# Who makes the sums of the down weights: GpSimd takes the four sums of each quarter, VectorE three low parts of each pass

## The reference

```
h = x + 0.5 * swiglu(rmsnorm(x), w_gate, w_up, w_down)          # first feed-forward stage
p = rmsnorm(h) @ w_in ; state-space group and short convolution  # mixer
h = h + concat(s_out, c_out) @ w_out
h = h + 0.5 * swiglu(rmsnorm(h), w_gate2, w_up2, w_down2)        # second feed-forward stage
y = rmsnorm(h)
swiglu(x, wg, wu, wd) = (silu(x @ wg) * (x @ wu)) @ wd           # inner width 2816
```

## Time and profile before

| | us |
|---|---|
| median of 3 runs | 1780.46 (1779.91 to 1780.72) |
| the profiled execution | 1779.56 |
| its span, first to last instruction | 1777.7 |
| TensorE busy | 1761.6 (99%), 11953 matmuls |
| VectorE busy | 1316.3 (74%), 2429 instructions |
| ScalarE busy | 652.3 (37%), 1281 instructions |
| GpSimd busy | 644.3 (36%), 669 instructions |
| granted clock of TensorE, mean | 0.998 |

### The profile page before, as it was taken

One profiled execution on the slowest core, in us unless ns is written; L12 is line 12 of the kernel. 1 busy time (PEld: TensorE's weight loads), 2 busy tenths in 40 slices (PEclk: granted clock), 3 DMA queues, 4 the chain that ended last, 5 costly groups with the idle time before them and its releaser, 6 DMA issues.

```text
span 1777.7 us, 31737 instructions
## 1 busy us (share of the span) xinstructions
PE 1761.6 (99%) x11953; PEld 1749.4 (98%) x11953; DVE 1316.3 (74%) x2429; ACT 652.3 (37%) x1281; POOL 644.3 (36%) x669
## 2 busy tenths in 40 slices
PE   8999999999999999999999999999999999999998
PEld 7999999999999999999999999999999999999998
DVE  7658878777877876823775769977887797788766
ACT  7411333333333333533112545333333333333324
POOL 2688232332333232203995221223233332323321
PEclk9999999999999999999999999999999999999999
DMA  6132111111111111355113501111111112111112
GB/s 174 36 131 84 54 54 48 55 48 57 46 54 54 48 54 43 143 128 128 48 42 110 174 14 54 47 56 48 54 48 54 54 43 60 48 54 48 54 49 96
DMA packets 162647, 119.75 MB, mean 67 GB/s; under 512 B 10258, under 2 KB 156242, under 8 KB 161988
## 3 DMA queue, kind: packets, MB, share of 16 engines
q1 hardware_dynamic: 157012, 110.10, 20.9%
q0 software_dynamic: 864, 5.28, 0.9%
q10 hardware_dynamic: 4624, 2.36, 0.6%
HBM read 102.01 MB, written 15.72 MB: 66 GB/s over the span
## 4 chain that ended last, share of the span: by engine, by line
PE 96%; DVE 2%; ACT 1%; issue 0%; DVEq 0%; POOL 0%; POOLq 0%
PE bank_pair L1128 26%; PE bank_pair L1130 25%; PE bank_pair L1129 25%; PE bank_down L1128 6%; PE bank_down L1130 6%; PE bank_down L1129 6%; DVE HT L2298 1%; DVE XL L2321 1%; PE bank_pair L1542 0%; PE bank_pair L1515 0%; PE bank_pair L1638 0%; PE bank_pair L1534 0%; PE bank_pair L1236 0%; PE bank_down L1278 0%; DVE S L2315 0%
## 5 line engine op out<-in xcount | busy, mean ns | idle before, releaser
L1128 PE MATMUL bank_pair<-XHM,U_hi 128*128 128x344 f32 x720 | 230.5, 320 | 0.2 <-DVE XLM L2343 0.2
L1129 PE MATMUL bank_pair<-XLM,U_hi 128*128 128x344 f32 x720 | 229.7, 319 | 0.0
L1130 PE MATMUL bank_pair<-XHM,U_lo 128*128 128x344 f32 x720 | 229.7, 319 | 0.0
L2549 DVE SCALAR_TENSOR_TENSOR HT<-bank_pair,HT 128x344 f32<-128x344 f32 x378 | 186.2, 508 | 51.0 <-PE bank_pair L1130 50.8
L3206 POOL TENSOR_TENSOR U_lo<-AST,U_hi 128x512 fp32r<-128x512 f32 x74 | 106.0, 1435 | 266.1 <-ACT U_hi L1702 266.1
L1128 PE MATMUL bank_pair<-XH,U_hi 128*128 128x344 f32 x608 | 194.1, 319 | 0.0
L1130 PE MATMUL bank_pair<-XH,U_lo 128*128 128x344 f32 x608 | 194.1, 319 | 0.0
L1129 PE MATMUL bank_pair<-XL,U_hi 128*128 128x344 f32 x608 | 194.0, 319 | 0.0
L1128 PE MATMUL bank_pair<-XH,WH 128*128 128x344 f32 x576 | 186.7, 324 | 5.0 <-DVE XL L2321 4.9
L1130 PE MATMUL bank_pair<-XH,WL 128*128 128x344 f32 x576 | 184.2, 320 | 0.0
L1129 PE MATMUL bank_pair<-XL,WH 128*128 128x344 f32 x576 | 184.2, 320 | 0.0
(11 more groups left out here) (398 smaller groups left out, 4922.7 us busy)
## 6 DMA issues: line engine op xcount, KB each, us to landing
DQ_raw<-in_ffn_w_down SPq DMA_DIRECT2D x52, 256.0 KB, 2.7
U_raw<-in_ffn_w_gate SPq DMA_DIRECT2D x40, 256.0 KB, 3.0
AST<-in_ffn_w_gate SPq DMA_DIRECT2D x40, 256.0 KB, 2.9
U_raw<-in_ffn_w_up SPq DMA_DIRECT2D x40, 256.0 KB, 3.3
AST<-in_ffn_w_up SPq DMA_DIRECT2D x40, 256.0 KB, 2.9
RAW<-in_w_in SPq DMA_DIRECT2D x16, 512.0 KB, 4.0
DQR<-in_ffn_w_down SPq DMA_DIRECT2D x25, 256.0 KB, 2.6
X<-in_x_prompt SPq DMA_DIRECT2D x8, 512.0 KB, 8.6
```

What stands on the lines that cost most here:

```text
L1128: pe.matmul(out, wh, xh, start=first, stop=False, skip_group_check=onto)
L1129: pe.matmul(out, wh, xl, start=False, stop=False, skip_group_check=onto)
L1130: return pe.matmul(out, wl, xh, start=False, stop=last, skip_group_check=onto)
L2549: dve.scalar_tensor_tensor(ht, STEP_BANKS[STEP_BANK[n]][:, 0:TW], 0.5, ht, ALU.mult, ALU.add).then_inc(pair_free, 1)
```

## The change

`mix_quarter` moves from VectorE's list to GpSimd's, with the same waits and semaphores. In return the low parts of A21, A22 and S4 move from GpSimd's list to VectorE's, in each of the 36 passes. In VectorE's even pass they stand at chunks 12 (A22) and 21 (S4), and at chunk 40 for the A21 of the coming odd pass; in its odd pass A22 stands behind `h_lo2(p, 0)` in M1, S4 behind the first product sum in M2, and the A21 of the coming even pass in M3. In GpSimd's list of the odd pass two quarters stand ahead of S1, one ahead of S4 and one behind it.

```diff
--- before.py
+++ after.py
@@ -2514,19 +2514,6 @@
                 hi, lo, raw = quarter(n)
                 dve.tensor_tensor(lo[:, :], raw[:, :], f(hi[:, :]), ALU.subtract).then_inc(dq_ready, 1)
 
-            def mix_quarter(n):
-                dve.wait_ge(dq_in[QUARTERS[n]], quarter_loads(n))
-                if n >= 2:
-                    dve.wait_ge(pair_full, sums_end(n - 2))
-                w = quarter(n)[2][:, :].rearrange("p (k m n) -> p k m n", k=2, m=2)
-                s, done = SR[n % 2], 4 * mixed_quarters(n)
-                dve.tensor_tensor(s[:, S1 - S1, :], w[:, 0, 1], w[:, 1, 1], ALU.add).then_inc(dq_mixed, 1)
-                dve.tensor_tensor(s[:, S3 - S1, :], w[:, 0, 0], w[:, 0, 1], ALU.subtract).then_inc(dq_mixed, 1)
-                dve.wait_ge(dq_mixed, done + 1)
-                dve.tensor_tensor(s[:, S2 - S1, :], s[:, S1 - S1, :], w[:, 0, 0], ALU.subtract).then_inc(dq_mixed, 1)
-                dve.wait_ge(dq_mixed, done + 3)
-                dve.tensor_tensor(s[:, S4 - S1, :], w[:, 1, 0], s[:, S2 - S1, :], ALU.subtract).then_inc(dq_mixed, 1)
-
             def sums_lo(n):
                 dve.wait_ge(ds_hi, mixed_quarters(n) + 1)
                 dve.tensor_tensor(SL[n % 2][:, :, :], SR[n % 2][:, :, :], f(SH[n % 2][:, :, :]), ALU.subtract
@@ -2644,32 +2631,34 @@
                                 quarter_lows(4 * p - 3)
                             if chunk == 11:
                                 unit_lo(t, S2)
+                            if chunk == 8 and t == FIRST[e] + 2:
+                                unit_lo(t, A21)
+                            if chunk == 12:
+                                unit_lo(t, A22)
                             if chunk == 13:
                                 unit_lo(t, S1)
-                            if chunk == 14:
-                                mix_quarter(4 * p - 2)
                             if chunk == 16:
                                 c11(t)
                             if chunk == 18:
                                 quarter_lows(4 * p - 2)
                             if chunk == 20:
                                 unit_lo(t, S3)
-                            if chunk == 23:
-                                mix_quarter(4 * p - 1)
+                            if chunk == 21:
+                                unit_lo(t, S4)
                             if chunk == 26:
                                 quarter_lows(4 * p - 1)
                             if chunk == 29:
                                 c22(t)
                             if chunk == 33:
                                 unit_lo(t + 1, A11)
-                            if chunk == 32 and p not in LAST_PAIR:
-                                mix_quarter(4 * p)
                             if chunk == 35:
                                 unit_lo(t + 1, S1)
                             if chunk == 37:
                                 c12(t)
                             if chunk == 39:
                                 unit_lo(t + 1, A12)
+                            if chunk == 40:
+                                unit_lo(t + 1, A21)
                             if chunk == 41 and p in LAST_PAIR:
                                 quarter_lo(4 * p)
                                 quarter_lo(4 * p + 1)
@@ -2677,17 +2666,17 @@
                         dve.wait_ge(pair_full, step_base(p))
                         for name in ORDER:
                             if name == "V1a":
-                                if p not in LAST_PAIR:
-                                    mix_quarter(4 * p + 1)
                                 unit_lo(t, S2)
                             if name == "V1b":
                                 mul(t, "V1b", "v", (0, 0))
                             if name == "M1":
                                 unit_lo(t, S3)
                                 h_lo2(p, 0)
+                                unit_lo(t, A22)
                             if name == "M2":
                                 c11(t)
                                 mul_sum(t, "C11", (0, 1))
+                                unit_lo(t, S4)
                                 if p not in LAST_PAIR:
                                     quarter_lows(4 * p)
                             if name == "M6" and p not in LAST_PAIR:
@@ -2774,7 +2764,6 @@
             mul_plain(0, 0)
             t_step(t_raw(0, T4), x_part(XH, b21), t_raw(0, T2), ALU.subtract, 5)
             t_step(t_raw(0, T4), t_raw(0, T4), x_part(XL, b21), ALU.add, 8)
-            mix_quarter(0)
             mul_plain(0, 1)
             h_lo2(0, 0)
             x_unit_lo(0, T3)
@@ -2789,7 +2778,6 @@
             h_lo2(0, 2)
             x_unit_lo(0, T2)
             h_lo2(0, 3)
-            mix_quarter(1)
             unit_lo(2, A12)
             mul_plain(0, 4)
             mix_h(0, T4)
@@ -2950,7 +2938,6 @@
             x_unit_lo(1, T1)
             mul_plain(1, 0)
             t_step(xr(T4), xr(T4), t_raw(1, T2), ALU.subtract)
-            mix_quarter(4 * PAIR0[1])
             mul_plain(1, 1)
             h_lo2(PAIR0[1], 0)
             x_unit_lo(1, T3)
@@ -2965,7 +2952,6 @@
             h_lo2(PAIR0[1], 2)
             x_unit_lo(1, T2)
             h_lo2(PAIR0[1], 3)
-            mix_quarter(4 * PAIR0[1] + 1)
             unit_lo(FIRST[1] + 2, A12)
             mul_plain(1, 4)
             mix_h(PAIR0[1], T4)
@@ -3206,15 +3192,45 @@
                 pool.tensor_tensor(UL[slot][:, :], raw[:, :], UH[slot][:, :].bitcast(F32), ALU.subtract
                                    ).then_inc(unit_ready[slot], 1)
 
+            def mix_quarter(n):
+                pool.wait_ge(dq_in[QUARTERS[n]], quarter_loads(n))
+                if n >= 2:
+                    pool.wait_ge(pair_full, sums_end(n - 2))
+                w = quarter(n)[2][:, :].rearrange("p (k m n) -> p k m n", k=2, m=2)
+                s, done = SR[n % 2], 4 * mixed_quarters(n)
+                pool.tensor_tensor(s[:, S1 - S1, :], w[:, 0, 1], w[:, 1, 1], ALU.add).then_inc(dq_mixed, 1)
+                pool.tensor_tensor(s[:, S3 - S1, :], w[:, 0, 0], w[:, 0, 1], ALU.subtract).then_inc(dq_mixed, 1)
+                pool.wait_ge(dq_mixed, done + 1)
+                pool.tensor_tensor(s[:, S2 - S1, :], s[:, S1 - S1, :], w[:, 0, 0], ALU.subtract).then_inc(dq_mixed, 1)
+                pool.wait_ge(dq_mixed, done + 3)
+                pool.tensor_tensor(s[:, S4 - S1, :], w[:, 1, 0], s[:, S2 - S1, :], ALU.subtract).then_inc(dq_mixed, 1)
+
             def ffn_passes(e):
+                mix_quarter(4 * PAIR0[e])
                 for t in range(FIRST[e] + 2, LAST_PASS[e] + 1):
-                    make(t, S1)
-                    make(t, S2)
-                    make(t, S3)
-                    make(t, S4)
-                    unit_lo(t, A21)
-                    unit_lo(t, A22)
-                    unit_lo(t, S4)
+                    p, g = divmod(t, 2)
+                    if t == FIRST[e] + 2:
+                        make(t, S1)
+                        make(t, S2)
+                        mix_quarter(4 * p - 3)
+                        make(t, S3)
+                        make(t, S4)
+                    elif g == 0:
+                        make(t, S1)
+                        make(t, S2)
+                        make(t, S3)
+                        make(t, S4)
+                    else:
+                        mix_quarter(4 * p - 2)
+                        mix_quarter(4 * p - 1)
+                        make(t, S1)
+                        make(t, S2)
+                        make(t, S3)
+                        if p not in LAST_PAIR:
+                            mix_quarter(4 * p)
+                        make(t, S4)
+                        if p not in LAST_PAIR:
+                            mix_quarter(4 * p + 1)
 
             ffn_passes(0)
             norm(1)
```

## The result

| | before | after |
|---|---|---|
| median | 1780.18 us (1779.84 to 1780.72, 6 runs) | 1786.82 us (1784.93 to 1787.87, 6 runs) |
| span of the profiled execution | 1777.7 us | 1785.3 us |
| TensorE busy | 1761.6 us | 1763.9 us |
| VectorE busy, instructions | 1316.3 us, 2429 | 1259.4 us, 2249 |
| GpSimd busy, instructions | 644.3 us, 669 | 622.3 us, 849 |

A forecast was written before the change was run, and what follows sets the result against it. TensorE, without idle time in the passes, was taken to bound the kernel; 1779.56 us of the profiled execution + 0 + 0 + 0 = 1779.6, or 1780.4 us against the median, no change; range 1778.5 to 1786.

The forecast's parts named there:

- What bounds it, and what could be won: Second feed-forward stage: TensorE busy 509.00 of 509.00 us, so the change can only leave it alone or make it wait.
- The exchange of work: VectorE loses 288 sums (120.8 us), gains 108 low parts (80); GpSimd loses about 156 us, gains about 153; TensorE 0.
- the relief: VectorE: without GpSimd's long low parts beside it, its instructions shorten; odd-pass queue ends 0.4 us earlier in M3.
- The queue of transfers, the tightest place: SyncE, odd passes: A11 issued 0.8 us later behind A22's refill; slack before M7 falls but holds, cost 0.
- rival A: Odd passes: A11 lands too late, ScalarE holds M6's copy, TensorE waits at M7; 1785 to 1801 us, chance 0.10.
- mild form: The late-A11 rival with landings after 3.9 us: 0.3 us in each of 16 odd passes, 5 us, 1785.

The follow-up runs named there:

- experiment 7: Changed kernel, with ScalarE making the high half `h_hi2(p, 0)` ahead of `sums_hi(4p+1)` in odd passes: 1784.49 us, ratio 1.0024 to before.
- experiment 2: Changed kernel, with ScalarE copying M6 before it makes the high part of the next A11 in odd passes: 1780.21 us, ratio 1.0001 to before.
- experiment 3: Changed kernel with the quarters' sums back on VectorE in their old places, so only the low parts move: 1783.36 us, ratio 1.002 to before.
- experiment 6: Changed kernel, with A22's low part in odd passes later on VectorE, behind the add and multiply of M2: 1860.03 us, ratio 1.0443 to before.
- experiment 1: Changed kernel, with A22's low part in odd passes earlier on VectorE, right behind that of S2: 1780.0 us, ratio 0.9999 to before.
- experiment 4: Kernel before, with only the quarters' sums moved to GpSimd, which keeps its low parts: 1779.86 us, ratio 1.0 to before.
- experiment 5: Changed kernel, with SyncE issuing the refill of A22 behind the next pass's A11 transfer, not ahead of it: 1780.22 us, ratio 1.0001 to before.

## Why the prediction was wrong

**What bounds it, and what could be won: right.** No idle time of TensorE in the passes, nothing won there.

**The exchange of work: right in its sizes.** GpSimd's 128x128 sums took 0.46 to 0.52 us in the mean of each group (I took 0.49 between bounds of 0.32 and 1.13), VectorE's busy time fell to 1259.4 us (1230 to 1275), GpSimd's total came to 622.3 us (near 644). GpSimd's list was in time for its own readers, S1 and the copy of M7. The low parts were taken for 0.743 us each and took 0.69. That the relief comes from a shared path is what the Trainium skill's "SBUF — State Buffer", section "Who interferes with whom", states; the shorter low parts agree, and TensorE's time did not depend on it.

**The failed step** is the one headed "The queue of transfers, the tightest place": "The slack falls from 1.1 us to 0.5 to 1.0 and holds: cost 0." Its order of events was right, and so was the place of A11 in it: I had it issued 4.66 us before M7, and it was 4.70 (1357.63 to 1362.33). Wrong was the landing. I took 2.7 to 3.2 us, the least and the median of all transfers into U_raw, for one that stands 0.4 us behind another; my slack of 0.5 to 1.0 us leaves the upper half of that row out. There it was 3.27 to 3.50 us in 13 passes and 4.17, 5.01 and 5.22 in three. Two things in the rows spoke against the median. The largest value was 6.9. And before, A11's high part started 3.38 us after its issue, so nothing had to be ready sooner. With 3.41 us, the copy of M6 behind it (0.54 later, for 0.44) and 0.14 from its end to TensorE, 0.17 us of slack are left, not 0.5 to 1.0. From there nearly the whole excess of a long landing is TensorE's loss.

What happened is rival A, which I had given 0.10, and in its mild form: it struck seven of 16 passes, by 0.1 to 1.7 us, for 6.5 us in all, where I had worked out 5 us for a small delay in each pass. That the two sums are close is luck: mine was 0.3 us in each of 16 passes, and nine passes lost nothing. The first condition that I gave, two transfers 0.4 us apart slowing each other, was the one to price. The second, VectorE late with A22, came true in four passes by a path that I had not followed (below). The Trainium skill's "DMA: Bandwidth & Descriptors", section "Rules for kernel authors", says that two transfers to disjoint halves of the partitions serialise, since both spread over the same 16 engines. The trace agrees for two whole transfers: in the pass that just holds they were issued 0.41 us apart and landed 0.81 us apart (1360.21 and 1361.02). That accounts for the 0.4 us by which A11 is slower behind the refill than alone, and not for the landings of 4.1 to 5.4 us. My argument against A, a queue that moves only 52 GB/s in this stretch, was a mean over 509 us; within 1.6 us three transfers of 256 KB stand in it.

**A step that I did not take.** "The refill of A21 for the next even pass also goes out some 3 us later (about 1343), with over 10 us left" is true of that refill, and I stopped there. Behind it on SyncE's queue stands the transfer of quarter 4p+1: issued at 307.45 before, at 312.17 after. Through the quarter's sums, `sums_hi` and `h_hi2(p, 0)` it reaches A22's low part again. I had the quarter's sums done in time for their own use, and did not ask who stands behind `sums_hi` on ScalarE. The trace puts 2.6 of the 6.5 us on this path, and experiment 7, which cuts it, gives back 2.3.

**What stays open: why a transfer behind another sometimes takes 4 to 5 us.** In the three windows where A11 took 4.17 to 5.22 us to land, one packet of an instruction queue lies among the data. All transfers around 1544 to 1550 us of the changed kernel (traffic in 40 slices, then the queues):

```profile
GB/s 0 0 0 0 0 0 0 22 71 63 48 130 253 309 350 346 320 339 343 462 309 279 250 190 194 287 246 246 261 175 93 60 30 19 19 19 22 19 19 19
...
q1 hardware_dynamic: 1575, 0.78, 50.0%
q8 instruction: 1, 0.02, 1.1%
```

The last seven slices, 1.0 us, move about 19 GB/s, where up to 462 were moved before, as if one of the 16 DMA engines were late with its share; from 1357 to 1363 there is no such packet and no such tail.

The traces of all nine kernels show how often this happens. A11 follows a refill by 0.4 us 80 times (the changed kernel and experiments 2, 3, 6 and 7, 16 odd passes each). By the landing itself, 11 of them took over 4 us, and in each of the 11 an instruction packet began 1.5 to 2.5 us after the issue: one of 16 KB where A11 took 4.56 to 5.20 us (8 times), one of 8 KB where it took 4.09 to 4.14 (3 times). The other 69 took 3.24 to 3.49 us; only two of them had a packet, and it began later, 2.95 and 3.04 us after the issue. Quarter 4p+1 follows a refill by 0.4 us 144 times; the 30 that took over 4 us all had a packet of 16 KB within 3.4 us of the issue (27 of them within 2.5 us). The other 114 took at most 3.97 us; ten of them had a packet, nine of these 2.5 us or more after the issue, the tenth of 8 KB.

A packet alone did not delay A11: where it stood alone (before and experiments 1 and 4, or ahead of the refill in experiment 5) it took at most 3.10 us in 64 passes, with a packet or without. Experiment 6 had no packet beside any A11, and its landings are all ordinary. So the long landings go with a transfer in front and an instruction packet beside it. That the packet is the cause is not shown: no run removed or moved one alone.

## What to carry to other kernels

When a step that frees a buffer moves, follow the queue of transfers behind its refill to its end, those of other tiles too, and see who waits behind each of them on every engine. Price a transfer that stands close behind another by its worst rows, not by the median; a slack that is under the difference is no cover. Where such a wait appears, the repair may be one line: the freeing step earlier, the other transfer first, or the copy that the busiest engine wants ahead of the work that waits for memory; each of the three gave the time of before, and none a better one, since TensorE had no idle time there to give.

## What was not expected of the hardware

A wait of TensorE of 2.8 to 3.0 us cost 1.3 to 2.8 us more behind it in 14 of 16 cases, by the clock at its 1.2 GHz level (experiment 6). The clock fell while TensorE still stood in eight of them and 0.8 to 1.5 us after it had started again in six. In the changed kernel the granted clock was 1.00 behind its waits of up to 1.5 us. So a wait of twice the length made TensorE later by up to 5.9 us instead of 1.7, 3.5 times as much.

The 128x128 sums took 0.46 to 0.52 us on GpSimd in the changed kernel, in the mean of each of eight groups, where VectorE's had ranged from 0.278 to 0.555 us. In experiment 4, where GpSimd keeps its low parts and VectorE makes none of the sums, two of the eight groups took 0.59 and 0.62 us. Why is open.
